# Six plain tiles instead of four ahead of the seven-product tiles, with the normalisation on VectorE

## What the reference computes

```
def rms_norm(x, g):
    y = x * rsqrt(mean(x * x, -1) + EPS)
    return y * g

def swiglu(h, w_gate, w_up, w_down):
    return (silu(h @ w_gate) * (h @ w_up)) @ w_down

for i in range(2):
    h = h + 0.5 * swiglu(rms_norm(h, norms[i, 0]), w_gate[i, 0], w_up[i, 0], w_down[i, 0])
    h = h + mix(rms_norm(h, norms[i, 1]))       # attention and state space, or sparse and differential attention
    h = h + 0.5 * swiglu(rms_norm(h, norms[i, 2]), w_gate[i, 1], w_up[i, 1], w_down[i, 1])
    h = h + sigmoid(rms_norm(h, norms[i, 3]) @ ple_w_gate[i]) * (p[i] @ ple_w_proj[i])
return rms_norm(h, final_norm)
```

## Time and profile before

| | us |
|---|---|
| median of 3 runs | 1955.7 (1955.67 to 1956.36) |
| the profiled execution | 1956.07 |
| its span, first to last instruction | 1954.2 |
| PE busy in the span | 1870.3 (96%) |
| DVE busy | 1383.3 (71%) |
| ACT busy | 901.8 (46%) |
| POOL busy | 328.7 (17%) |
| mean granted clock of TensorE | 0.981 |

### The profile page before, as it was taken

How to read it: one execution, slowest core, us unless ns; L and a number is a source line. 1 busy time by engine, 2 the same in 40 slices (tenths; PEclk the granted TensorE clock), 3 DMA queues, 4 the chain that set the end, 5 groups by cost and what they waited for, 6 DMA issues and landing times.

```text
span 1954.2 us, 32127 instructions
## 1 busy us (share of the span) xinstructions
PE 1870.3 (96%) x11562; PEld 1630.6 (83%) x11562; DVE 1383.3 (71%) x1982; ACT 901.8 (46%) x1523; POOL 328.7 (17%) x227
## 2 busy tenths in 40 slices
PE   6899999999979999999799999999989979999998
PEld 5799988777779998887599998877657779998886
DVE  5888888774788875347888873369984888875345
ACT  5555542245455554224455553234573455554222
POOL 4000001122500000224200000162243400000225
PEclk9899999999989999999899999999989989999999
DMA  3233333332223333322233332231101223333321
GB/s 141 77 107 107 107 103 108 86 110 82 71 70 107 107 105 111 107 85 77 74 98 107 107 118 97 97 116 65 54 1 44 87 68 104 107 107 119 108 76 54
DMA packets 56743, 179.74 MB, mean 92 GB/s; under 512 B 12144, under 2 KB 12144, under 8 KB 56656
## 3 DMA queue, kind: packets, MB, share of 16 engines
q1 hardware_dynamic: 54656, 173.69, 27.6%
q0 software_dynamic: 928, 3.02, 0.5%
q10 hardware_dynamic: 1088, 2.10, 0.3%
HBM read 175.04 MB, written 3.15 MB: 91 GB/s over the span
## 4 chain that ended last, share of the span: by engine, by line
PE 61%; DVE 9%; ACT 2%; issue 1%; POOL 0%; DVEq 0%; ACTq 0%
PE ps L2127 28%; PE ps L2094 18%; PE ps L2076 8%; PE ps L2568 2%; PE ps L2231 1%; DVE rstd L437 1%; DVE w_lo L380 1%; PE ps L2467 1%; DVE t L453 1%; DVE xs_lo L557 1%; ACT w_hi L372 1%; DVE sm L1169 1%; PE ps L2517 1%; PE ps L2486 0%; DVE work L1145 0%
## 5 line engine op out<-in xcount | busy, mean ns | idle before, releaser
L380 DVE TENSOR_TENSOR w_lo<-raw,w_hi 128x1024 fp32r<-128x1024 f32 x166 | 238.1, 1445 | 232.7 <-ACT w_hi L372 232.1
L2127 PE MATMUL ps<-xs_hi,w_hi 128*128 128x256 f32 x1152 | 327.4, 284 | 0.0
L2127 PE MATMUL ps<-xs_lo,w_hi 128*128 128x256 f32 x1152 | 327.2, 284 | 0.0
L2127 PE MATMUL ps<-xs_hi,w_lo 128*128 128x256 f32 x1152 | 327.1, 284 | 0.0
L372 ACT ACTIVATE w_hi<-raw 128x1024 fp32r<-128x1024 f32 x178 | 185.9, 1054 | 302.4 <-PE ps L2094 254.1
L2127 PE MATMUL ps<-x_hi,w_hi 128*128 128x256 f32 x864 | 247.3, 286 | 41.0 <-DVE x_lo L557 41.0
L2094 PE MATMUL ps<-act_hi,w_hi 128*128 (+1 forms) x720 | 280.3, 389 | 0.0
L2094 PE MATMUL ps<-act_lo,w_hi 128*128 (+1 forms) x720 | 280.1, 389 | 0.0
L2094 PE MATMUL ps<-act_hi,w_lo 128*128 (+1 forms) x720 | 280.1, 389 | 0.0
L2076 PE MATMUL ps<-x_hi,w_hi 128*128 128x512 f32 x576 | 234.8, 408 | 22.5 <-DVE w_lo L380 9.6
L499 DVE TENSOR_TENSOR w_lo<-w_sum,w_hi 128x1024 fp32r<-128x1024 f32 x144 | 175.9, 1222 | 104.9 <-ACT w_hi L1643 104.9
(11 more groups left out here) (399 smaller groups left out, 3270.8 us busy)
## 6 DMA issues: line engine op xcount, KB each, us to landing
raw<-in_weights SPq DMA_DIRECT2D x322, 512.0 KB, 3.5
h<-in_xT ACTq DMA_DIRECT2D x4, 512.0 KB, 6.5
out<-result SPq DMA_DIRECT2D x4, 512.0 KB, 3.0
p_raw<-in_pT POOLq DMA_DIRECT2D x2, 512.0 KB, 4.0
scratch_u<-u_sc SPq DMA_DIRECT2D x1, 512.0 KB, 6.4
u_grp<-scratch_u SPq DMA_DIRECT2D x1, 512.0 KB, 4.2
scratch_y<-y_grp SPq DMA_DIRECT2D x2, 256.0 KB, 3.2
y_ch<-scratch_y SPq DMA_DIRECT2D x1, 512.0 KB, 3.5
```

Of the source, the lines that this page charges most:

```text
L380: dve.tensor_tensor(w_lo[:, slot], raw[:, slot], w_hi[:, slot].bitcast(F32), SUB)\
L2127: last = pe.matmul(ps[:, bank, 0:HALF], w[:, at, cols], x[:, k], start=(start and k == 0 and part == 0), stop=(stop and k == KH - 1 and pa ...
```

## The change

PLAIN goes from 4 to 6: twelve plain chunks and 16 fast tiles in each block. The six plain tiles take the bank pairs (0,1), (2,3), (5,6), (0,1), (2,3), (0,1). The normalisation of `xn` moves from two instructions of 128x2048 on GpSimd to four of 128x1024 on VectorE. Residual number 4 gets a place of its own (`corner_hi`, `corner_lo`), and the semaphore `x_passed` goes. The activations of the plain tiles go to `act_f` and are split later: tiles 0 and 1 in the last fast tile, tiles 2 to 5 at the first step of the down projection. The orders of the lists of VectorE and ScalarE around the plain tiles are rewritten; in blocks 1 and 3 a fifth weight chunk is split before `root`, in block 0 a sixth, and in blocks 0 and 2 `root` comes ahead of `gained`.

```
-PLAIN = 4
+PLAIN = 6
+PLAIN_BANKS = ((0, 1), (2, 3), (5, 6), (0, 1), (2, 3), (0, 1))
...
+        corner_hi = over("corner_hi", [P, KH, HALF], at_hi + 2 * tile_bytes, F32R)
+        corner_lo = over("corner_lo", [P, KH, HALF], at_hi + 4 * tile_bytes, F32R)
...
+        def act_low(dve, f, t):
+
+            dve.wait_ge(ffn_sems["act_hi_ready"], t + 1 + NF * f)
+            span = slice(t * T, (t + 1) * T)
+            dve.tensor_tensor(act_lo[:, span], act_f[:, span], act_hi[:, span].bitcast(F32), SUB)\
+               .then_inc(ffn_sems["act_ready"], 1)
+
+        def tiles_split(j):
+
+            return range(2 if j == 0 else 4 + 2 * j, min(6 + 2 * j, NF))
+
...
+            def gate(t):
+                dve.wait_ge(chunk_used, first + 2 * t + 1)
+                dve.tensor_tensor(t1[:, t % 2], ps[:, PLAIN_BANKS[t][0]], rstd[:], MULT)\
+                   .then_inc(s["gate_scaled"], 1)
+
+            def up(t):
+                dve.wait_ge(chunk_used, first + 2 * t + 2)
+                dve.tensor_tensor(t2[:, t % 2], ps[:, PLAIN_BANKS[t][1]], rstd[:], MULT)\
                    .then_inc(s["up_scaled"], 1)
-                dve.wait_ge(s["up_scaled"], i * 2 + (b + 1) + NF * f)
-                dve.wait_ge(s["silu_done"], i * 2 + (b + 1) + NF * f)
-                dve.tensor_tensor(t2[:, b], t2[:, b], t1[:, b], MULT).then_inc(s["prod_done"], 1)
-
-            def low(i, b):
-                dve.wait_ge(s["act_hi_ready"], i * 2 + (b + 1) + NF * f)
-                span = bass.ds((i * 2 + b) * T, T)
-                dve.tensor_tensor(act_lo[:, span], t2[:, b], act_hi[:, span].bitcast(F32), SUB)\
-                   .then_inc(s["act_ready"], 1)
-
-            def two_tiles(i, peeled=False):
-                split_lo(dve, first, AHEAD, i)
-                split_lo(dve, first, AHEAD + 1, i)
-                if peeled and n == 0:
-                    split_lo(dve, first, AHEAD + 2, i)
-                if peeled:
-                    reciprocal_root(dve, n)
-                gate(i, 0)
-                if not peeled or n:
-                    split_lo(dve, first, AHEAD + 2, i)
-                up(i, 0)
-                split_lo(dve, first, AHEAD + 3, i)
-                gate(i, 1)
-                low(i, 0)
-                up(i, 1)
-                low(i, 1)
+
+            def plain_product(t):
+                dve.wait_ge(s["up_scaled"], t + 1 + NF * f)
+                dve.wait_ge(s["silu_done"], t + 1 + NF * f)
+                dve.tensor_tensor(act_f[:, t * T:(t + 1) * T], t2[:, t % 2], t1[:, t % 2], MULT)\
+                   .then_inc(s["prod_done"], 1)
+
+            def normalised(pair):
+                rows = slice(2 * pair, 2 * pair + 2)
+                dve.wait_ge(fast["x_gained"], KD * f + 2 * pair + 2)
+                dve.tensor_tensor(xn[:, rows], xn[:, rows],
+                                  rstd[:].unsqueeze(1).to_broadcast([P, 2, T]), MULT)\
+                   .then_inc(fast["x_normed"], 1)
...
-                dve.wait_ge(fast["x_normed"], 2 * f + 2)
+                dve.wait_ge(fast["x_normed"], 4 * f + 4)
...
+                elif o == 4:
+                    dst, src, hi = corner_lo[:], quarter(xn, o), corner_hi[:]
...
                 if down:
                     split_lo(dve, first, FFN_UP + 1)
+                    for t in range(2):
+                        act_low(dve, f, t)
                 up_left(i, b)
                 product(i, b)
...
-            two_tiles(0, peeled=True)
+            split_lo(dve, first, 2)
+            split_lo(dve, first, 3)
+            if n != 4:
+                split_lo(dve, first, 4)
+            if n == 0:
+                split_lo(dve, first, 5)
+            reciprocal_root(dve, n)
+            gate(0)
+            up(0)
+            normalised(0)
+            normalised(1)
+            if n == 4:
+                split_lo(dve, first, 4)
+            if n:
+                split_lo(dve, first, 5)
+            plain_product(0)
+            normalised(2)
+            normalised(3)
+            gate(1)
+            up(1)
             split_lo(dve, first, 6)
+            plain_product(1)
             split_lo(dve, first, 7)
-            weight_sums(2, 0)
             residual_sums()
-            for o in range(4):
-                residual_lo(o)
-            own_lo(2, 0, 0)
-            gate(1, 0)
-            up(1, 0)
-            sums_lo(2, 0, 1)
-            gate(1, 1)
-            low(1, 0)
-            sums_lo(2, 0, 0)
-            for o in range(4, 7):
-                residual_lo(o)
-            up(1, 1)
-            own_lo(2, 0, 1)
-            low(1, 1)
+            gate(2)
+            up(2)
+            residual_lo(0)
+            residual_lo(1)
+            plain_product(2)
+            split_lo(dve, first, 8)
+            residual_lo(2)
+            residual_lo(3)
+            split_lo(dve, first, 9)
+            residual_lo(4)
+            gate(3)
+            up(3)
+            split_lo(dve, first, 10)
+            plain_product(3)
+            weight_sums(3, 0)
+            split_lo(dve, first, 11)
+            own_lo(3, 0, 0)
+            gate(4)
+            up(4)
+            sums_lo(3, 0, 1)
+            plain_product(4)
+            gate(5)
+            sums_lo(3, 0, 0)
+            up(5)
+            residual_lo(5)
+            plain_product(5)
+            own_lo(3, 0, 1)
+            residual_lo(6)
...
-                    for t in range(PLAIN + 2 * j, min(PLAIN + 2 * j + 2, NF)):
-                        act_low(t)
+                    for t in tiles_split(j):
+                        act_low(dve, f, t)
...
-        def normalised(pool, f, n):
-            pool.wait_ge(rstd_ready, n + 1)
-            for half in range(2):
-                rows = slice(KH * half, KH * half + KH)
-                pool.wait_ge(fast["x_gained"], KD * f + KH * half + KH)
-                pool.tensor_tensor(xn[:, rows], xn[:, rows],
-                                   rstd[:].unsqueeze(1).to_broadcast([P, KH, T]), MULT)\
-                    .then_inc(fast["x_normed"], 1)
...
-            normalised(pool, 0, 0)
...
+        def act_high(act, f, t, first=None):
+
+            span = slice(t * T, (t + 1) * T)
+            act.wait_ge(ffn_sems["prod_done"], t + 1 + NF * f)
+            if t >= 2:
+                act.wait_ge(chunk_used, first - 1)
+            act.activation(act_hi[:, span], act_f[:, span], ACT.Copy)\
+               .then_inc(ffn_sems["act_hi_ready"], 1)
...
-                        act.wait_ge(fast["x_passed"], (KD - 1) * f + KH)
+                        act.wait_ge(fast["x_normed"], 4 * f + 4)
+                        dst = corner_hi[:]
                     else:
                         act.wait_ge(chunk_used, first + 2 * PLAIN)
-                    dst, src = (quarter(a, o) for a in (x_hi, xn))
+                        dst = quarter(x_hi, o)
+                    src = quarter(xn, o)
...
-            two_tiles(0, peeled=True)
+            if split:
+                split_hi(act, first, 2)
+                split_hi(act, first, 3)
+            if n == 4:
+                root(act, n)
+                gained(range(KH))
+                split_hi(act, first, 4)
+                gained(range(KH, KD))
+            elif n:
+                split_hi(act, first, 4)
+                gained(range(KD))
+                root(act, n)
+            else:
+                split_hi(act, first, 4)
+                split_hi(act, first, 5)
+                root(act, n)
+                gained(range(KD))
+            silu(0)
+            if n:
+                split_hi(act, first, 5)
             split_hi(act, first, 6)
+            silu(1)
             split_hi(act, first, 7)
             for o in range(4):
                 residual_hi(o)
-            own_hi(2, 0, 0)
-            silu(2, 0)
-            sums_hi(2, 0, 1)
-            product_hi(2, 0)
-            silu(3, 1)
-            sums_hi(2, 0, 0)
-            for o in range(4, 7):
-                residual_hi(o)
-            own_hi(2, 0, 1)
-            product_hi(3, 1)
+            silu(2)
+            split_hi(act, first, 8)
+            split_hi(act, first, 9)
+            residual_hi(4)
+            silu(3)
+            split_hi(act, first, 10)
+            split_hi(act, first, 11)
+            own_hi(3, 0, 0)
+            silu(4)
+            sums_hi(3, 0, 1)
+            silu(5)
+            sums_hi(3, 0, 0)
+            residual_hi(5)
+            own_hi(3, 0, 1)
+            residual_hi(6)
...
-                if j >= 4:
-                    pe.wait_ge(s[("gate_scaled", "up_scaled")[j % 2]], j // 2 - 1 + NF * f)
-                in_chunk(pe, first, j, j % 4, n=n if j == 0 else None,
-                         freed=fast["x_passed"] if j == 2 * PLAIN - 1 else None)
+                t, half = divmod(j, 2)
+                before = [e for e in range(t) if PLAIN_BANKS[e] == PLAIN_BANKS[t]]
+                if before:
+                    pe.wait_ge(s[("gate_scaled", "up_scaled")[half]], before[-1] + 1 + NF * f)
...
```

(42 more changed lines are left out.)

25 lines of the change are left out of this document (2 added, 23 removed).

## The result

| | us |
|---|---|
| before, median of 4 runs | 1955.93 (1955.67 to 1956.36) |
| after, median of 4 runs | 1904.06 (1903.32 to 1904.31) |
| ratio after/before, 95% interval | 0.9734 (0.9717 to 0.9751) |
| span of the profiled execution | 1902.3, before 1954.2 |
| mean granted clock of TensorE | 0.997, before 0.981 |

A forecast was written before the change was run, and what follows sets the result against it. TensorE, 96% busy, was taken to lose time mainly waiting for VectorE's late list. Block gains of 17.1, 10.1, 12.8 and 11.3 (51.3) bring span 1954.2 to 1902.9, execution 1904.8, median 1904.5 us; range 1893 to 1914.

The forecast's parts named there:

- The long wait at the entry: First fast tile's waits for residual_lo, 41.0 us in four blocks, go; in block 1 residual 4 is 23 us early.
- Price of a plain tile: Each plain tile replacing a fast one costs 10.88 - 10.08 = 0.80 us, 6.4 us for 8.
- The normalisation on VectorE: Each new 128x1024 operation on VectorE's list takes 1.15 us, four making 4.6; at most 2.5 each.
- rival (c): Plain stretch: VectorE becomes late, plain chunks wait 3 to 5 us a block, about 1920 us; chance 0.13.
- The entry wait: After the last plain chunk: copy 0.25 us late, sums_lo wait 1.1 in tile 2; 1.35 us a block, bounds 0 and 3.
- a sign of being right: The first fast tile of a block would take about 10.3 us at clock 1.00.
- The exit wait: First down matmul waits for act_low of tiles 0 and 1: 1.3 us a block, bounds 0.5 and 2.
- GpSimd's squares: An extra VectorE split among the sums of squares delays TensorE 0.9 us in blocks 0 and 1; bounds 0 and 2.3.
- The blocks: Chunk 4 to first down matmul takes 207.45 us; blocks 0 to 3 gain 17.1, 10.1, 12.8, 11.3, sum 51.3.
- (b): The small waits at entry, exit and squares are covered: 1894 us; chance 0.09.
- (d): Fast loop: VectorE's late turn exceeds 10.08 us, so every tile pays; slower, 1968 us at 11.1; chance 0.03.
- (e): First fast product still waits, for a weight's split, half as long as before: 1934 us; chance 0.01.

The follow-up runs named there:

- no_corner: The changed kernel with residual 4 written over x_hi and x_lo again and split after the last plain chunk has passed: 1903.71 us.
- pool_norm: The changed kernel with the normalisation back on GpSimd, all else as changed: 1903.65 us.
- before_norm: The kernel before with only its normalisation moved to VectorE, four instructions behind up(0): 1943.57 us.
- plain4: The changed kernel with four plain tiles instead of six, lists shortened and their order slightly different: 1915.76 us.
- plain8: The changed kernel with eight plain tiles instead of six, first fast tile's preparation moved behind them: 1910.0 us.
- rotate: The changed kernel with the next tile's weight sums made one step earlier on VectorE, tile 7's ahead of up(5): 1898.83 us.
- early_act: The changed kernel with activations of plain tiles 0 and 1 split at the start of the last fast tile, ahead of the down weights' splits: 1898.46 us.
- late_split: The changed kernel with the extra weight split of blocks 0, 1 and 3 put behind the root and first normalisations: 1901.56 us.
- plain4_gate: The changed kernel with four plain tiles, gate(3) ahead of residual 4, earlier split of activations 0 and 1, later extra weight split: 1904.76 us.
- double_norm: The changed kernel with each of the four VectorE normalisations followed by one more operation of the same size: 1906.92 us.

## Why the prediction was right, and where it was not

**The long wait at the entry goes, the main term: right.** Residual 4 was split 23.2 us early (23 predicted), and the first tile runs at clock 1.00. The experiments add what the prediction did not say. The wait stays gone without the place of residual 4 (no_corner), without the move of the normalisation (pool_norm) and without both; and that move alone does not end it (before_norm). With four tiles and all other parts (plain4) it is gone too, and 40 of the 52 us are there, though in block 0 the same product then waits 3.48 us for a weight. What every kernel without the wait has is the third bank pair and the rewritten lists; which line of them does it was not tried singly, and no run adds two plain tiles to the kernel before and nothing else. So that VectorE's list was late is shown; what puts it in time is shown only for the set.

**Price of a plain tile, 0.80 us: right.** In plain8 each block up to its first down matmul takes 1.6 us more, the 2 x 0.80 booked; its whole span is 7.1 longer, its median 5.9, where 6.4 was expected.

**The normalisation on VectorE, 1.15 us: right** (1.14 start to start). Four times 1.14 more in every block cost 2.6 us in all, so rival (c) is out: the slack on the list is real (the booked 5 us of idle time are the 2.46 and 2.52 before up(4) and gate(5)), smallest in block 0. The Trainium skill (SBUF — State Buffer, section Who interferes with whom) says that a VectorE instruction with two SBUF inputs contends with a GpSimd one that reads SBUF, and that one with a single SBUF input does not, outside its 2-port modes. This case's rows agree: 5.09 us for a product of 0.68, while L464, which reads PSUM and one SBUF operand, took 0.68 in the same stretch. The prediction said that the rule speaks for the move; here the move was worth nothing, and 12.6 us only in the kernel whose list had no room.

**The entry wait, 1.35 us: right in cause and size, wrong in place.** The 0.25 us booked at product 3 measured 0.28. The prediction put 1.1 us more at the second product of tile 2, for the second `sums_lo`. It came two products earlier, before the last product of tile 1, 0.90 us and 0.2 behind it, and the releaser is a copy on ScalarE. So the first tile took 559.57 - 548.18 = 11.4 us, not the 10.3 that was named as a sign of being right. Its timeline shows why:

```profile
555.65 1.06 ACT L1648 ACTIVATE w_hi<-w_sum 128x1024 fp32r<-128x1024 f32 x1 [2.31 <-DVE w_sum L493]
556.62 1.04 ACT L1638 ACTIVATE w_hi<-raw 128x1024 fp32r<-128x1024 f32 x1
557.57 0.36 ACT L1654 ACTIVATE part_sum<-ps 128x256 f32<-128x256 f32 x1
```

The late weight sum, as predicted, holds ScalarE 2.31 us, and the copy stands two instructions behind. Tile 2 then starts late enough for `sums_lo` to be in time. rotate, which only moves the weight sums, ends it.

**The exit wait, 1.3 us: right.** VectorE at the end of block 1:

```profile
709.54 1.23 DVE L383 TENSOR_TENSOR w_lo<-raw,w_hi 128x1024 fp32r<-128x1024 f32 x1
710.68 1.28 DVE L447 TENSOR_TENSOR act_lo<-act_f,act_hi 128x512 fp32r<-128x512 f32 x2
```

The splits end at 711.96, TensorE goes at 712.07. It lost 1.21 us a block, as early_act shows, which gave back 4.6 of the span.

**GpSimd's squares, 0.9 us in blocks 0 and 1: right.** Chunk 4 of block 1 came 0.8 us later than the gain of block 0 alone puts it: 43.5 before 548.18, that is 504.7, against 520.86 - 17.0 = 503.9. late_split gave back 1.6 by then, blocks 0 and 1 together, and 2.5 of the span. GpSimd's additions show the same; the six of block 0, before and after:

```profile
15.53 11.10 POOL L1428 TENSOR_TENSOR sumsq<-sumsq,first_sq 128x512 f32<-128x512 f32 x6
```

```profile
15.84 11.89 POOL L1459 TENSOR_TENSOR sumsq<-sumsq,first_sq 128x512 f32<-128x512 f32 x6
```

They take 0.79 us more, and the last of block 1 0.84 more (2.13 against 1.29): the booked 0.9 a block holds, and nothing shows the larger price of the full 1.14 us. Of the rest of late_split's gain 0.2 us is an earlier first weight and 0.8 lies in the mixer behind block 2: a stretch of TensorE there takes 10.15 us at a granted clock of 0.84 (1383.22 to 1393.37) where after took 10.98 at 0.71 (1385.00 to 1395.98). No run shows that the edit has a part in that.

**The blocks.** Entry to exit took 163.9 us in each, 161.3 + 2.65 = 163.95 was booked. The gains were 17.0, 10.2, 12.7 and 11.9 us, forecast 17.1, 10.1, 12.8 and 11.3, each the earlier first down matmul less what the blocks before had given: for block 1, 739.32 - 712.07 - 17.01 = 10.24. The 0.6 us more of block 3 is not explained. In block 2 nothing of chunk 4's split is seen in the waits.

**The rivals.** (b), (c), (d) and (e) are all refused by the same trace: both small waits are there, no chunk of 4 to 11 waits, a tile takes 10.08 us, and the first fast product goes without a wait. Three expectations behind the prediction missed: plain4 came 8 us, plain4_gate 2 us and double_norm 0.9 us above the upper end that my theory gave them.

## What to carry to other kernels

Price a set of edits as a set: the normalisation's move was worth 12.6 us alone and nothing in company, for the rewritten lists and the longer plain stretch give VectorE slack enough either way. When a producer on one engine is late, follow the in-order list of every engine that waits for it, for the wait shows where some other, innocent instruction stands behind. And when a longer cheap stretch gives a late engine time to catch up, add to it until the waits are gone and no further: four, six and eight tiles gave 1915.8, 1904.1 and 1910.0 us. Part of the first number was a badly placed `gate(3)`: give each count its own best order before you compare.

## What was not expected of the hardware

TensorE's granted clock falls to its lower level after idle times much shorter than the 11.10 us of before, and not each time after the same one. First block 0 of plain4_gate, which begins behind an idle time of 5.13 us:

```profile
60.14:63.20 3.06, 3.06 (x14) 3.06 (x15) 3.06 (x4) 0.68 (x2) 0.00 (x0) 0.50 0.52 170
...
63.20:70.00 6.80, 6.80 (x58) 6.80 (x57) 5.67 (x7) 2.17 (x5) 0.00 (x0) 0.99 0.25 80
```

Then plain4: block 0 behind 3.48 us, blocks 1 and 2 behind 2.25 us each (in block 2 the idle time ended at 948.01).

```profile
59.39:62.40 3.01, 3.01 (x14) 3.01 (x15) 3.01 (x4) 0.24 (x1) 0.00 (x0) 0.50 0.54 174
62.40:65.40 3.00, 2.48 (x12) 2.18 (x11) 1.95 (x3) 3.00 (x6) 0.00 (x0) 0.50 0.02 5
537.60:540.00 2.40, 2.40 (x20) 2.40 (x21) 2.40 (x4) 0.61 (x2) 0.00 (x0) 1.00 0.19 27
949.49:952.90 3.41, 3.41 (x18) 3.41 (x18) 2.86 (x4) 0.83 (x2) 0.00 (x0) 0.50 0.46 154
```

After 5.13 us of idle, 3.06 us at 0.50 (1.2 GHz) hold 14 matmuls, 0.21 us each where 0.12 is usual: about 1.3 us lost (14 x 0.09). After 3.48 us, less, the clock stays at 0.50 longer, for all 24 matmuls of the first two products, the last at 64.46: about 2.2 us lost (24 x 0.09). After 2.25 us it goes either way: it stays at 1.00 in block 1, and in block 2 it falls 1.5 us behind the restart. In the fast stretches of after, behind waits of about 1 us, it stays at 1.00. So these runs give no idle time from which on the clock falls, and the cost of a wait beyond itself does not follow from its length.
